# Half a tile of tokens moved from matmuls over all experts to dots over fetched rows

## The chip, the cores and the metric

The kernel runs on one core of one Trainium2 chip. The metric is the device time of one execution, in microseconds. An execution computes one transformer layer over 512 tokens.

## The reference

The layer mixes 512 tokens of 1024 features with four kinds of attention, normalises, and then runs an expert layer (PEER) with 16384 experts, each one row of `u` and one row of `v`. Each token picks 16 experts in each of 8 heads, 128 in all, through two lists of 128 subkeys:

```python
s_top, i_top = lax.top_k(sub, PEER_TOPK)                 # 16 of 128, in both halves of a head
cand = s_top[:, :, 0, :, None] + s_top[:, :, 1, None, :]
sc, ci = lax.top_k(cand.reshape(t_len, PEER_HEADS, 256), PEER_TOPK)
eid = (i1 * N_KEYS + i2).reshape(t_len, 128)
gate = jax.nn.softmax(sc, axis=-1).reshape(t_len, 128)
...
h = jax.nn.gelu(jnp.einsum('cd,ced->ce', xc, u[ec]), approximate=False)
return jnp.einsum('ce,ced->cd', gc * h, v[ec])
```

The result is normalised once more. The change concerns the expert layer alone.

## The kernel before

**Data.** Tokens lie in four tiles of 128. Weights come in units of 128 x 1024 numbers (0.524 MB). SP loads each unit into one of four slots of `raw` (`load_unit`); ScalarE rounds it to `w_hi` (`split_hi`, L539); GpSimd or DVE takes the remainder `w_lo` (L486, L1055). TensorE makes three matmuls of each product, high by high, high by low and low by high.

**The expert layer in two halves.** For tiles 1 to 3 (384 tokens) the kernel computes all 16384 experts. First half: 128 units of `u`, each eight chunks by three matmuls with 384 token columns (`project`, L1285 to L1287) into PSUM bank 0 or 1 in turn. ScalarE applies gelu from there (`gelu_of`) and stores the result to the DRAM scratch `gelu_d`. Second half: 128 units of `v` (`value_unit`, `add_tile`, L1511 to L1514), for each tile six matmuls with 512 columns. Their stationary operand is gate times gelu, which DVE multiplies (`times_gelu`) from `gate_in` and `gelu_in` as they come back from DRAM, and which is split again (`gh_high` on ScalarE, `gh_low` on DVE).

For tile 0 only the chosen experts are computed. GpSimd fetches rows of `u` by index (`get_u`, 128 rows of 4 KB a fetch, 0.524 MB), DVE multiplies each by the token's x, which stands in PSUM banks 6 and 7, and sums (`dot`, L1061): 128 dots in the first half. In the second half rows of `v` are fetched (`get_v`) and added with their weights (`fma`, L1073).

**The gates.** DVE picks the experts of a tile (`route`: runs of MAX8, FIND_INDEX8, MATCH_REPLACE8, then a selection in PSUM banks 2 to 5). TensorE turns the picks (`turn_picks`), DVE copies them (`spread_picks`, L1169). Then the tile goes four tokens (a quad) at a time: DVE builds two indicator matrices `left` and `match` of 128 x 512 (`mark`, L1179 and L1180), DVE or, for three quads of four, ScalarE makes `right` from `match` and the gates, TensorE multiplies them per token (`gates_of`, L1609), ScalarE copies the 128 x 128 gates of four tokens to `stage` (`take_gates`, L731), and after eight quads stores 2 MB of them to `gate_d` (`store_gates`, L738).

**Order.** Every engine's order is written out by hand, along the 128 units of the first half: 16 units alone, then three times (tiles 1, 2, 3) 14 units during which the tile is routed and 16 units in which two quads follow each unit, then 22 units of tail. `dots_by` says how many dots are done by which unit: 3, 6, 6 in the routing stretches, 30 in each marking stretch, 23 in the tail. DVE does the marks of a unit, then the dots due by it, in one order; GpSimd does a unit's split, then the fetches due (up to five dots ahead, one buffer each). A fetch waits until the dot that used its buffer is done. In the tail SP starts to reload the gates at unit 120 (`load_gates`), after the last store has landed.

## Time and profile before

| | |
|---|---|
| median of 3 runs | 1729.89 us (1728.78 to 1734.46) |
| the profiled execution | 1732.18 us |
| its span, first to last instruction | 1730.4 us |
| TensorE busy | 1689.1 us (98%) |
| VectorE (DVE) busy | 1255.8 us (73%) |
| ScalarE (ACT) busy | 768.7 us (44%) |
| GpSimd (POOL) busy | 820.7 us (47%) |
| moved by DMA | 417.65 MB, mean 241 GB/s |
| first half of the expert layer | about 580 to 1197 us |
| second half | 1197 to 1718 us |

Busy time is an average over stages with different limits, so the stages are read one by one. Matmul durations in the profile are modelled and overlap; the pace is read from one start to the next. Idle time of an engine that isn't the bound costs nothing; what it waited for tells what would be late next. The granted TensorE clock is 1.00 (2.4 GHz) in all stretches of the expert layer.

### The profile page before, as it was taken

Reading aid. Unit: us, or ns where it says so; the run is one execution under the profiler, and the core shown is the slowest. Engines: PE = TensorE matmul, PEld = TensorE weight load, DVE = VectorE, ACT = ScalarE, POOL = GpSimd, SP = SyncE. Lnnn points to the kernel's source line nnn. Section 1 sums busy time; section 2 is a strip of 40 time slices with the busy share of each in tenths; the row PEclk is TensorE's granted clock in tenths of the full one; section 3 lists DMA queues with packets and bytes.
Section 4 is the critical chain, followed back from the end, with each engine's and each line's share of the span. In section 5 each row is a group of like instructions: output and inputs, shape, how many; then the busy total and the mean of one; then the engine's idle time right before and its main releaser. Section 6 shows DMA issues by size and latency. Waiting matters only on the chain.

```text
span 1730.4 us, 24570 instructions
## 1 busy us (share of the span) xinstructions
PE 1689.1 (98%) x9061; PEld 1486.3 (86%) x9061; DVE 1255.8 (73%) x2490; ACT 768.7 (44%) x1301; POOL 820.7 (47%) x496
## 2 busy tenths in 40 slices
PE   7999999999999999999999999999999999999997
PEld 6667767778878999999999999999888888888886
DVE  2487896562353778789888987534888888888886
ACT  4444444522232443775577367534333333333332
POOL 5222222344446466766777677776433232332312
PEclk9999999999999999999999999999999999999998
DMA  5111111224233365899799789997999999999952
GB/s 200 61 62 50 59 60 54 77 94 146 84 112 110 113 197 186 306 372 345 253 333 384 249 286 386 383 364 296 405 390 354 384 376 351 383 372 354 389 190 85
DMA packets 126360, 417.65 MB, mean 241 GB/s; under 512 B 12961, under 2 KB 32417, under 8 KB 124705
## 3 DMA queue, kind: packets, MB, share of 16 engines
q1 hardware_dynamic: 70176, 232.81, 38.2%
...
## 4 chain that ended last, share of the span: by engine, by line
PE 88%; DVE 8%; ACT 2%; issue 1%; DMA 1%; POOL 0%; SPq 0%; another core or an unknown queue 0%; ACTq 0%; DVEq 0%; POOLq 0%
PE ps L1285 16%; PE ps L1287 16%; PE ps L1286 16%; PE ps L1514 11%; PE ps L1511 11%; PE ps L1512 11%; PE ps L1609 5%; PE ps L1370 1%; DVE dist_a L842 1%; DVE row L895 1%; DVE row L866 1%; DVE small L841 1%; PE ps L1395 1%; DVE small L892 1%; DMA raw<-w_units 0%
## 5 line engine op out<-in xcount | busy, mean ns | idle before, releaser
L1285 PE MATMUL ps<-tok_hi,w_hi 128*128 128x384 f32 (+2 forms) x1544 | 548.8, 355 | 8.4 <-issue 3.6
L1287 PE MATMUL ps<-tok_hi,w_lo 128*128 128x384 f32 (+2 forms) x1544 | 539.3, 349 | 0.0
L1286 PE MATMUL ps<-tok_lo,w_hi 128*128 128x384 f32 (+2 forms) x1544 | 539.3, 349 | 0.0
L539 ACT ACTIVATE w_hi<-raw 128x1024 fp32r<-128x1024 f32 x334 | 353.3, 1058 | 414.0 <-PE ps L1514 301.4
L486 POOL TENSOR_TENSOR w_lo<-raw,w_hi 128x1024 fp32r<-128x1024 f32 x128 | 318.2, 2489 | 165.8 <-ACT w_hi L539 165.2
L439 POOL TENSOR_TENSOR w_lo<-raw,w_hi 128x1024 fp32r<-128x1024 f32 x80 | 195.0, 2442 | 327.0 <-ACT w_hi L539 326.8
L1285 PEld LDWEIGHTS ps<-tok_hi,w_hi 128*128 128x128 f32 x1544 | 291.1, 189 | 35.7 <-issue 10.2
L1287 PEld LDWEIGHTS ps<-tok_hi,w_lo 128*128 128x128 f32 x1544 | 290.8, 188 | 18.6
L1286 PEld LDWEIGHTS ps<-tok_lo,w_hi 128*128 128x128 f32 x1544 | 291.3, 189 | 16.8
L1511 PE MATMUL ps<-w_hi,gh_hi 128*128 128x512 f32 x768 | 298.8, 389 | 0.0
L1512 PE MATMUL ps<-w_lo,gh_hi 128*128 128x512 f32 x768 | 298.8, 389 | 0.0
L503 POOL DMA_INDIRECT v_got<-v_rows,eid x128 | 150.4, 1175 | 303.6 <-DVE own L1073 286.7
L1514 PE MATMUL ps<-w_hi,gh_lo 128*128 128x512 f32 x768 | 236.5, 389 | 0.0
L1061 DVE CUSTOM_DVE_ANT_0 u_got<-u_got,ps 128x1024 f32<-128x1024 f32 x128 | 153.3, 1217 | 90.5 <-DMA u_got<-u_rows,eid 88.0
L1055 DVE TENSOR_TENSOR w_lo<-raw,w_hi 128x1024 fp32r<-128x1024 f32 x126 | 156.3, 1241 | 74.0 <-ACT w_hi L539 73.4
L1514 PEld LDWEIGHTS ps<-w_hi,gh_lo 128*128 128x128 f32 x768 | 144.2, 188 | 29.9
L1512 PEld LDWEIGHTS ps<-w_lo,gh_hi 128*128 128x128 f32 x768 | 144.2, 188 | 29.9
L1511 PEld LDWEIGHTS ps<-w_hi,gh_hi 128*128 128x128 f32 x768 | 144.2, 188 | 29.8
L1073 DVE SCALAR_TENSOR_TENSOR own<-v_got,w_own,own 128x1024 f32<-128x1024 f32 x126 | 159.8, 1278 | 0.0
L495 POOL DMA_INDIRECT u_got<-u_rows,eid x128 | 123.1, 961 | 27.7 <-issue 20.4
L706 ACT ACTIVATE gelu_t<-ps 128x384 f32<-128x384 f32 x120 | 58.7, 489 | 173.3 <-PE ps L1287 151.5
L1609 PE MATMUL ps<-right,left 128*128 128x128 f32 x768 | 93.5, 275 | 0.5 <-ACT right L722 0.5
...
## 6 DMA issues: line engine op xcount, KB each, us to landing
raw<-u_units SPq DMA_DIRECT2D x128, 512.0 KB
raw<-v_rows SPq DMA_DIRECT2D x128, 512.0 KB
...
gelu_d<-gelu_t ACTq DMA_DIRECT2D x120, 192.0 KB
...
```

Of the source, the lines that this page charges most:

```text
L439: pool.tensor_tensor(w_lo[:, n % RAW, :], raw[:, n % RAW, :], w_hi[:, n % RAW, :].bitcast(F32), ALU.subtract).then_inc(lo_done, 1)
L486: pool.tensor_tensor(w_lo[:, n % RAW, :], raw[:, n % RAW, :], w_hi[:, n % RAW, :].bitcast(F32), ALU.subtract).then_inc(lo_pool, 1)
L539: act.activation(w_hi[:, n % RAW, :], raw[:, n % RAW, :], ACT.Copy).then_inc(hi_done, 1)
L1055: dve.tensor_tensor(w_lo[:, n % RAW, :], raw[:, n % RAW, :], w_hi[:, n % RAW, :].bitcast(F32), ALU.subtract).then_inc(lo_dve, 1)
L1073: dve.scalar_tensor_tensor(own[e % 2][:], v_got[e % V_SLOTS][:], w_own[:, e:e + 1], own[e % 2][:], ALU.mult, ALU.add).then_inc(fma_done, 1)
L1285: pe.matmul(out_, l_hi, r_hi, start=start, stop=False)
L1286: pe.matmul(out_, l_hi, r_lo, start=False, stop=False)
L1287: return pe.matmul(out_, l_lo, r_hi, start=False, stop=stop)
L1511: pe.matmul(o, l_hi[:, tile_], wh, start=start, stop=False)
L1512: pe.matmul(o, l_hi[:, tile_], wl, start=False, stop=False)
L1514: last = pe.matmul(o, l_lo[:, tile_], wh, start=False, stop=stop)
L1609: last = pe.matmul(ps[:, 2 + q % 3, t * P:(t + 1) * P], left[:, s, t, :], right[:, s, t, :], start=True, stop=True)
```

## The change

The first 64 tokens of tile 1 (`NEAR`) leave the first half's matmuls, which now have 320 columns (`UT`). Their h is computed by dots instead. Two groups of 64 experts lie on the two halves of the partitions, so 64 more dots cover 64 tokens times 128 experts; 192 dots in all (`DOTS`). Their indices, x rows and results are spread and brought back by six small DMAs on ScalarE's queue (`spread_near_eid`, `spread_near_x`, `finish_near`). The x in PSUM is exchanged before dot 42 and again before dot 106 (`take_x`). The gates of these tokens are multiplied by their gelu (`weigh_near`) and marked last, after tile 3, for which their picks are kept and turned a fourth time; the second half then multiplies them by ones (`gelu_in[:, :, 0:NEAR]`), since it still covers all three tiles.

The order is new. 14 units alone, then three times 18 units of routing, and 9, 17 and 25 units of marking with 16, 32 and 48 quads; a tail of 9 units. Dots: 8, 10, 10 in routing, 22, 44, 68 in marking, 6 in the tail, 24 in the first 16 units of the second half (`late_dots_by`). Fetches may use three buffers before the ninth dot, then five, and six in the middle (`slots_at`, `dot_slots`). Two quads are marked in one instruction with 1024 elements. In the second half, one unit of four is split by GpSimd instead of DVE (`by_pool`), the fmas start at unit 18 instead of 2 and end at 118 instead of 116, and tile 3 is summed in banks 0 and 1, as banks 6 and 7 hold x. The first reload of gates stands behind the last `u` unit, its second part behind the second `v` unit.

```diff
-FIRST_UNITS, ROUTE_UNITS, MARK_UNITS = 16, 14, 16
-TAIL = FIRST_UNITS + 3 * (ROUTE_UNITS + MARK_UNITS)
-ROUTE_DOTS, MARK_DOTS = (3, 6, 6), 30
-U_SLOTS, V_SLOTS = 5, 6
-FMA_START, FMA_END = 2, P - 12
+NEAR = 2 * TOK
+UT = DT - NEAR
+NEAR_GROUPS = P // NEAR
+DOTS = P + NEAR
+FIRST_UNITS, ROUTE_UNITS, MARK_UNITS = 14, 18, (9, 17, 25)
+TAIL = FIRST_UNITS + 3 * ROUTE_UNITS + sum(MARK_UNITS)
+ROUTE_DOTS, MARK_DOTS, TAIL_DOTS, LATE_DOTS = (8, 10, 10), (22, 44, 68), 6, 24
+NEAR_FROM, NEAR_END = 42, 42 + NEAR
+assert sum(ROUTE_DOTS) + sum(MARK_DOTS) + TAIL_DOTS + LATE_DOTS == DOTS
+U_SLOTS, V_SLOTS = 6, 6
+FMA_START, FMA_END = LATE_DOTS * 2 // 3 + 2, P - 10
...
+def routed_at(b):
+
+    return FIRST_UNITS + (b - 1) * ROUTE_UNITS + sum(MARK_UNITS[:b - 1])
+
+
+def first_quad(b):
+
+    return max(0, 32 * (b - 1) - NEAR // 4) if b < NT else N_QUAD
+
+
+def tile_quad(q):
+
+    r = q + NEAR // 4
+    return r // 32 + 1, r % 32
+
+
+def quads_of(b, k):
+
+    first, count = first_quad(b), first_quad(b + 1) - first_quad(b)
+    return range(first + count * k // MARK_UNITS[b - 1], first + count * (k + 1) // MARK_UNITS[b - 1])
+
+
+def pairs_of(b, k):
+
+    return [q for q in quads_of(b, k) if q % 2 == 0]
...
+def stretch_dots():
+
+    by = [0] * FIRST_UNITS
+    for b in range(1, NT):
+        for units, dots in ((ROUTE_UNITS, ROUTE_DOTS[b - 1]), (MARK_UNITS[b - 1], MARK_DOTS[b - 1])):
+            by += [by[-1] + dots * (k + 1) // units for k in range(units)]
+    units = P - TAIL
+    return by + [by[-1] + TAIL_DOTS * (k + 1) // units for k in range(units)]
...
+DOTS_BY = stretch_dots()
+NEAR_UNIT = next(k for k in range(P) if DOTS_BY[k] >= NEAR_END) + 3
+
+
+def dot_row(d):
+
+    if NEAR_FROM <= d < NEAR_END:
+        return True, d - NEAR_FROM
+    return False, d if d < NEAR_FROM else d - NEAR
...
+def slots_at(d):
+
+    return 3 if d < ROUTE_DOTS[0] else U_SLOTS if SIX_FROM <= d < SIX_END else U_SLOTS - 1
...
+def fmas_by(j):
+
+    return max(0, min(P, P * (j - FMA_START + 1) // (FMA_END - FMA_START)))
+
+
+def late_dots_by(j):
+
+    return min(DOTS, DOTS - LATE_DOTS + 3 * (j + 1) // 2)
+
+
+DOT_SLOTS = dot_slots()
+
+
+def by_pool(j):
+
+    return j + LO_AHEAD < P and j % 4 == 1
...
+                j = n - first - P
+                if by_pool(j):
+                    engine.wait_ge(lo_pool, P + sum(by_pool(i) for i in range(j + 1)))
+                else:
+                    engine.wait_ge(lo_dve, sum(not by_pool(i) for i in range(j + 1)))
+
+    def ffn_bank(t):
+
+        return {1: 2, 2: 4, 3: 0}[t]
...
             for j in range(P):
                 load_unit(U_EXP + j, u_units[j])
-                if j == P - 8:
-                    sp.wait_ge(gate_read, N_QUAD)
-                    for s in range(2):
-                        sp.wait_ge(stage_out[s], 16 * (NB // 2))
-                    load_gates(0, 0)
-                if j == P - 4:
-                    load_gates(0, 1)
+            sp.wait_ge(gate_read, N_QUAD)
+            for s in range(2):
+                sp.wait_ge(stage_out[s], 16 * (NB // 2))
+            load_gates(0, 0)
             for j in range(P):
                 load_unit(U_VAL + j, v_rows[:, (j - KEPT) % P, :])
+                if j == 1:
+                    load_gates(0, 1)
...
+                if k == P - 8:
+                    pool.wait_ge(pick_set, NT)
+                    pool.wait_ge(dot_done, SIX_END)
+                    for i in range(2):
+                        pool.memset(gelu_in[i][:, :, 0:NEAR], 1.0).then_inc(ones_set, 1)
+                if k < FIRST_UNITS + ROUTE_UNITS:
+                    rows_to(min(DOTS_BY[k - 1] + 3, ROUTE_DOTS[0]))
+                else:
+                    done = DOTS_BY[k - 1]
+                    rows_to(done + slots_at(done))
             for s in range(2):
...
-            for e in range(P):
-                get_v(e)
+            sent = 0
+            for j in range(P):
+                if by_pool(j):
+                    expert_lo(P + j)
+                rows_to(late_dots_by(j) + U_SLOTS - 1)
+                while sent < min(P, fmas_by(j - 1) + V_SLOTS):
+                    get_v(sent)
+                    sent += 1
             pool.wait_ge(ln2_in, 32)
...
+            def spread_near_eid():
+
+                act.wait_ge(near_set, 1)
+                for g in range(NEAR_GROUPS):
+                    part = slice(NEAR * g, NEAR * g + NEAR)
+                    act.dma_start(near_eid[part, :], near_all[0:NEAR, part]).then_inc(near_eid_in, 16)
+
+            def spread_near_x():
+
+                act.wait_ge(pick_set, 3)
+                for g in range(NEAR_GROUPS):
+                    act.dma_start(near_x[NEAR * g:NEAR * g + NEAR, :], x_tok[0:NEAR, 1, :]).then_inc(near_x_in, 16)
+
+            def finish_near():
+
+                act.wait_ge(dot_done, NEAR_END)
+                act.activation(near_dot[:], near_dot[:], ACT.Gelu).then_inc(near_gelu, 1)
+                act.wait_ge(near_gelu, 1)
+                for g in range(NEAR_GROUPS):
+                    part = slice(NEAR * g, NEAR * g + NEAR)
+                    act.dma_start(near_h[0:NEAR, part], near_dot[part, :]).then_inc(near_h_in, 16)
 
             for k in range(FIRST_UNITS):
                 expert_unit(k)
@@ -750,17 +884,25 @@
...
+            def take_x(rows, n):
+
+                dve.wait_ge(dot_done, n)
+                dve.tensor_copy(ps[:, 6:8, :].rearrange("p a n -> p (a n)"), rows).then_inc(own_x, 1)
+                dve.wait_ge(own_x, 2 if n == NEAR_FROM else 3)
...
+            def keep_near():
+
+                dve.wait_ge(pick_set, 2)
+                dve.scalar_tensor_tensor(near_all[:], pick[:, 0, :], float(NK), pick[:, 1, :], ALU.mult, ALU.add)\
+                    .then_inc(near_set, 1)
+                dve.tensor_copy(near_keys[:], pick[:, 0:2, :])
+                settled(dve.tensor_copy(near_gate[:], pick[:, 2, :]))
+
+            def weigh_near():
+
+                dve.wait_ge(near_h_in, 16 * NEAR_GROUPS)
+                dve.tensor_tensor(near_gate[0:NEAR, :], near_gate[0:NEAR, :], near_h[0:NEAR, :], ALU.mult)\
+                    .then_inc(near_pick, 1)
+
...
             def mark(q):
 
-                s, quad = q % 4, q % 32
+                b, quad = tile_quad(q)
                 if q >= 4:
-                    dve.wait_ge(gate_full, q - 3)
-                first, second, gate = (ps[:, 5, a * P + 4 * quad:a * P + 4 * quad + 4].unsqueeze(2).to_broadcast([P, 4, P])
-                                       for a in range(3))
-                numbers = iota[:].unsqueeze(1).to_broadcast([P, 4, P])
-                dve.tensor_tensor(left[:, s, :, :], numbers, first, ALU.is_equal)
-                dve.tensor_tensor(match[:, s, :, :], numbers, second, ALU.is_equal).then_inc(match_set, 1)
-                if right_by(q)[0] == "dve":
-                    dve.wait_ge(match_set, q + 1)
-                    dve.tensor_tensor(right[:, s, :, :], match[:, s, :, :], gate, ALU.mult).then_inc(right_dve, 1)
+                    dve.wait_ge(gate_full, q - 2)
+                first, second = (ps[:, 5, a * P + 4 * quad:a * P + 4 * quad + 8].unsqueeze(2).to_broadcast([P, 8, P])
+                                 for a in range(2))
+                numbers = iota[:].unsqueeze(1).to_broadcast([P, 8, P])
+                two = slice(q % 4, q % 4 + 2)
+                dve.tensor_tensor(left[:, two, :, :].rearrange("p s t k -> p (s t) k"), numbers, first, ALU.is_equal)
+                dve.tensor_tensor(match[:, two, :, :].rearrange("p s t k -> p (s t) k"), numbers, second, ALU.is_equal)\
+                    .then_inc(match_set, 1)
+                if right_by(q + 1)[0] == "dve":
+                    gate = ps[:, 5, 2 * P + 4 * quad + 4:2 * P + 4 * quad + 8].unsqueeze(2).to_broadcast([P, 4, P])
+                    dve.wait_ge(match_set, q // 2 + 1)
+                    dve.tensor_tensor(right[:, 3, :, :], match[:, 3, :, :], gate, ALU.mult).then_inc(right_dve, 1)
 
             def times_gelu(j):
 
@@ -1189,6 +1366,8 @@
...
+                for k in range(MARK_UNITS[b - 1]):
                     expert_unit(routed_at(b) + ROUTE_UNITS + k)
-                    for quad in (2 * k, 2 * k + 1):
-                        gates_of(32 * (b - 1) + quad)
+                    for quad in quads_of(b, k):
+                        if b == NT - 1 and tile_quad(quad) == (NT, 0):
+                            turn_picks(NT)
...
-                tokens = slice(P, S) if n >= U_EXP else slice(0, S)
-                to = ps[:, bank, 0:DT] if n >= U_EXP else ps[:, bank, :]
+                tokens = slice(P + NEAR, S) if n >= U_EXP else slice(0, S)
+                to = ps[:, bank, 0:UT] if n >= U_EXP else ps[:, bank, :]
...
+                if b == NT:
+                    pe.wait_ge(near_pick, 1)
+                    pe.wait_ge(match_set, (N_QUAD - NEAR // 4) // 2)
+                    pe.wait_ge(right_dve, (N_QUAD - NEAR // 4) // 4)
+                    pe.wait_ge(gate_full, N_QUAD - NEAR // 4)
+                else:
```

## Rows read from the trace of the kernel before

**Rows 1.** The page's chain that ended last, shares by engine and by line

```profile
PE 88%; DVE 8%; ACT 2%; issue 1%; DMA 1%; POOL 0%; SPq 0%; another core or an unknown queue 0%; ACTq 0%; DVEq 0%; POOLq 0%
PE ps L1285 16%; PE ps L1287 16%; PE ps L1286 16%; PE ps L1514 11%; PE ps L1511 11%; PE ps L1512 11%; PE ps L1609 5%; PE ps L1370 1%; DVE dist_a L842 1%; DVE row L895 1%; DVE row L866 1%; DVE small L841 1%; PE ps L1395 1%; DVE small L892 1%; DMA raw<-w_units 0%
```

**Rows 2.** Groups of instructions by shape (count, busy us, mean ns), TensorE

```profile
L1285 PE MATMUL ps<-tok_hi,w_hi 128*128 128x384 f32 x1024 | 346.5, 338 | 0.0
```

**Rows 3.** Timeline (start us, us), TensorE: 256-column matmuls, then the first of 384

```profile
532.09 0.28 PE L1287 MATMUL ps<-tok_hi,w_lo 128*128 128x256 f32 x1
...
540.01 0.28 PE L1287 MATMUL ps<-tok_hi,w_lo 128*128 128x256 f32 x1
...
580.49 0.34 PE L1285 MATMUL ps<-tok_hi,w_hi 128*128 128x384 f32 x1
```

**Rows 4.** The chain in order of time (start us, us): marking, first value matmul

```profile
724.43 1.78 PE ps L1609 x16
...
795.79 1.78 PE ps L1609 x16
...
1196.88 0.23 PE ps L1511
```

**Rows 5.** Windows: PE, PEld, DVE, ACT, POOL busy, granted clock, DMA share, GB/s

```profile
712.00:800.00 88.00, 87.75 (x591) 87.75 (x592) 77.44 (x156) 62.88 (x143) 65.20 (x45) 1.00 0.98 376
...
1020.00:1108.00 88.00, 88.00 (x595) 88.00 (x594) 72.44 (x122) 62.81 (x142) 63.45 (x44) 1.00 0.96 361
...
1400.00:1600.00 200.00, 200.00 (x884) 165.64 (x883) 171.22 (x203) 72.24 (x98) 61.76 (x55) 1.00 0.99 369
```

**Rows 6.** The same view in windows of 20 us

```profile
1020.00:1040.00 20.00, 20.00 (x141) 20.00 (x140) 19.38 (x34) 15.16 (x35) 14.09 (x11) 1.00 0.87 290
1040.00:1060.00 20.00, 20.00 (x134) 20.00 (x134) 14.22 (x25) 14.15 (x32) 13.82 (x11) 1.00 1.00 389
1060.00:1080.00 20.00, 20.00 (x137) 20.00 (x136) 17.41 (x31) 14.91 (x36) 14.53 (x10) 1.00 1.00 393
...
1140.00:1160.00 20.00, 20.00 (x117) 20.00 (x116) 6.21 (x12) 5.53 (x8) 16.10 (x11) 1.00 1.00 371
...
1240.00:1260.00 20.00, 20.00 (x89) 16.54 (x89) 17.85 (x23) 8.71 (x12) 10.48 (x7) 1.00 1.02 405
```

**Rows 7.** Groups of instructions, DVE, 1020 to 1108 us, with idle before

```profile
L1061 DVE CUSTOM_DVE_ANT_0 u_got<-u_got,ps 128x1024 f32<-128x1024 f32 x30 | 35.8, 1215 | 15.3 <-DMA u_got<-u_rows,eid 15.2
```

**Rows 8.** Timeline of DVE: two mark steps, a dot, routing of tile 2

```profile
789.20 0.68 DVE L1179 TENSOR_TENSOR left<-iota,ps 128x512 f32<-128x512 f32 x1
789.80 0.68 DVE L1180 TENSOR_TENSOR match<-iota,ps 128x512 f32<-128x512 f32 x1
...
793.45 1.22 DVE L1061 CUSTOM_DVE_ANT_0 u_got<-u_got,ps 128x1024 f32<-128x1024 f32 x1
...
794.60 3.19 DVE L1083 MAX8 s_top<-sub 128x8 f32<-128x128 f32 x16
...
850.62 0.29 DVE L1160 TENSOR_TENSOR pick<-pick,g_sum 128x128 f32<-128x128 f32 x1
856.19 0.29 DVE L1169 COPY g_T<-ps 128x128 f32<-128x128 f32 x1 [5.28 <-PE ps L1598]
```

**Rows 9.** Groups of instructions, GpSimd, 1020 to 1108 us

```profile
L486 POOL TENSOR_TENSOR w_lo<-raw,w_hi 128x1024 fp32r<-128x1024 f32 x15 | 36.1, 2404 | 18.2 <-ACT w_hi L539 18.1
L495 POOL DMA_INDIRECT u_got<-u_rows,eid x29 | 27.4, 944 | 6.4 <-issue 4.6
```

**Rows 10.** Timeline of ScalarE around the last store of gates

```profile
1111.26 0.33 ACTq L738 DMA_DIRECT2D gate_d<-stage  x1
...
1113.93 0.33 ACTq L708 DMA_DIRECT2D gelu_d<-gelu_t  x1
...
1124.42 0.49 ACT L706 ACTIVATE gelu_t<-ps 128x384 f32<-128x384 f32 x1 [4.85 <-DMA gelu_d<-gelu_t]
```

**Rows 11.** Groups of instructions, DVE, 1200 to 1400 us

```profile
L1055 DVE TENSOR_TENSOR w_lo<-raw,w_hi 128x1024 fp32r<-128x1024 f32 x50 | 61.1, 1223 | 28.2 <-ACT w_hi L539 27.6 <-issue 0.6
```

199 lines of the change are left out of this document (122 added, 77 removed).

## The prediction

> **What bounds the kernel now.** I read the chain of work that ended last first [rows 1]: 88% of the span is TensorE, and the lines of the two expert halves (L1285 to L1287, L1511 to L1514, L1609) carry nearly all of it. So a shorter TensorE stream is worth its whole length, until another engine is late. Then the rates of the matmuls. Their durations in the groups of instructions [rows 2] are modelled and overlap, so I take start to start: 0.120 us at 256 columns in the same line of code [rows 3] (66 matmuls from 532.09 to 540.01), and 200/884 = 0.226 at 512 columns [rows 5]. For 384 columns the chain gives 5.947 us for a unit with eight gate matmuls (12 periods from 724.43 to 795.79) [rows 4]; less 1.78 for the gates that is 4.165, or 0.1735 us for each of 24. The three lie on one line, 0.42 ns a column. Last, who is close behind. In the stretches in which gates are marked, DVE is busy 77.4 of 88 us, and the DMA engines 0.96 to 0.98 of the time at 361 to 376 GB/s [rows 5]; already there dots wait 15.3 us for fetched rows in 88 us [rows 7]. The kernel is bound by TensorE, with DMA at its heels in just the stretches to which the change adds transfers.
>
> **What the change takes off TensorE.** 3 x 1024 matmuls [rows 2] go from 384 to 320 columns: 0.1735 - 64 x 0.00042 = 0.147 us, 3.52 us a unit for 4.165. 128 units x 0.64 = 82 us. The 96 quads of gate matmuls stay (0.89 each, 85 us); three transposes more are 0.5 us. Before, the last first-half unit ends at 1196.88 [rows 4]; TensorE alone would bring that to 1115. The second half (18 matmuls of 512 columns, 4.07 us a unit) keeps its length.
>
> **DVE.** Dots cost 1.14 us from their start to that of the next instruction (793.45 to 794.60, read of the sum and all) [rows 8]. 64 are added and 24 of the 192 lie in the second half, so 168 instead of 128 in the first: +46 us. A mark step is 0.60 us for 512 elements, start to start (789.20 to 789.80) [rows 8]; at 1.04 ns an element (0.53) a step of 1024 costs 1.13, so the joined steps save 0.07 x 96 = 6 us. Route: from the first MAX8 at 794.60 to the last of pick at 850.9 is 56.3, of which 6 dots are 6.9 [rows 8]; 49.4 without. With 8, 10, 10 dots: 59, 61, 61 us; 18 units of TensorE are 63.4, so routing stays just hidden. The three mark stretches have 16, 32, 48 quads, 22, 44, 68 dots, and 9, 17, 25 units. A pair of quads is 2.27, right for every second pair 0.7 more: DVE needs 46, 92 and 141 us, plus some 2.5 us each in the last two for copying the new x rows (1.2 each) and the picks of the late tokens. TensorE needs 9 x 3.52 + 16 x 0.89 = 46, 88 and 131. So DVE becomes some 16 us longer than TensorE over these. Adding up from 580.49 (first 384-column unit after unit 0) [rows 3], less 0.6: unit 31 ends at 689; marks to 736; route to 799; marks to 895; route to 959; marks to 1103; nine units of tail 32: 1135 by DVE. To that comes one hand-over that the trace of before has only at the start of a mark stretch: at the 33rd quad of the third stretch DVE waits in spread_picks until TensorE has finished the 17 units and 32 quads before and one unit more and turned the picks of the late tokens (all marks and dots behind it wait too), then TensorE waits for the first new right. Before, DVE stood 5.3 us at the like place [rows 8], where it had run ahead; I take 4, bounds 0 and 7: 1139.
>
> **The other new waits and small DMAs.** near_eid, near_x and near_h are two small transfers each on ScalarE's queue, 0.33 us an issue [rows 10], 2 us over 450. finish_near holds ScalarE (behind it: the next split and gelu, and so TensorE's banks) until 106 dots are done, but it stands three units, 16 us, after they are planned, and near_h has nine units to arrive before weigh_near. Nothing, as long as dots are less than 16 us late. The first copy of near_x waits for all dots before it, which is DVE's own order. SP's gate reload moves from unit 120 to behind the last u unit; by the tail's account below it couldn't run earlier.
>
> **GpSimd.** A split is 2.40, a gather's issue 0.94 and some 0.2 of idle between issues [rows 9]. A mark unit with 2.7 dots: 2.40 + 2.7 x 1.15 = 5.5 us, where TensorE has 5.24 and DVE 5.6. It is a third resource at the same length, on no path by itself. Its in-order waits for dot_done hold the next split, but a split is two units ahead, 10 us.
>
> **DMA.** From 689, when rows after the eighth can be fetched, to the end of the first half, must move: 93 units of u and 4 of v (50.9 MB, 0.524 each), 160 gathers (83.9), gelus of 88 units at 0.164 (14.4), the gates out (25.2) and the first of them in (3.1), x rows 0.5: 178 MB. What does DMA carry? Fully busy 20 us windows moved 389 and 393 GB/s in marking, 371 in the tail, 405 in the second half [rows 6]; whole stretches 361 to 376 [rows 5]. I take 390, that of the same mixture, since in the long stretches part of the time was ramp (290 GB/s at 1020 to 1040 [rows 6]). 178/0.390 = 456 us, which ends at 1145. Two route stretches can't fill it: each has some 22.4 MB for 62 us, 57 at 390, so 9 us more. Row waits that DVE can't hide now that it has no slack: 8 us, an estimate of half of one stretch's 15.3 [rows 7], and 2 for the hand-over, where transfers run on; bounds 0 and 1/6 of the mark time (48). End of the first half: 1164. So DMA, not TensorE, is late: a mark unit has 2.56 MB, 6.6 us at 390 against 5.24.
>
> The tail shrinks from 22 units (92 us) to nine (32 us), with the last gate store and the gates' reload in it. A gelu store queued behind the gate store of 1111.26 frees its buffer at 1124.4, so a store takes ScalarE's queue some 12 us [rows 10]. After it the reload (3.1 MB, 8 us at full rate, 16 at half), then gh, its high and low parts (2 us): 22 to 30 us after ACT's last take, which lies 28 us before the end. It is inside the 178 MB; beyond it I take 1 us, bounds 0 and 12. The same store holds gelu buffers when units are 3.5 us long: two banks cover 10.6 us of those 12.
>
> **Second half.** By bytes, the first 16 units have 0.524 + 1.5 x 0.524 + 0.164 + 0.197 = 1.67 MB in 4.07 us, 410 GB/s, later ones 382 (before: 370). At 400, 1.6 us late; at the 369 of today's second half [rows 5], which is its demand and perhaps not its limit, 7 us. DVE there: per unit 1.5 dots (1.7), 0.75 of a split (1.22 [rows 11], 0.9), two half-microsecond steps: 3.6 of 4.07. The splits on GpSimd are needed two units later, 8 us, so nothing. The gate tile waits for banks 0 and 1 once, under 1 us. Together I take +3 us, bounds 0 and 17.
>
> **Sum** against the profiled execution, 1732.2 us (span 1730.4; the median of the runs is 2.3 lower): 1165 for 1197 is -32, second half +3: 1703. I keep that number; the 2.3 is below what I can resolve.
>
> The DMA rate is the doubtful term, and a rule speaks against mine. Fully busy windows here moved 371 to 405 GB/s on one core [rows 6]. The Trainium skill (HBM Reference, Specifications (TRN2)) has some 358 GB/s as a core's effective share of memory bandwidth, and more for a core alone. By 358 the first half would end at 689 + 497 + 10 = 1196, no gain at all; by its single-core figure of about 425 (same section), 689 + 419 + 19 = 1127, under DVE's 1139. The windows are all above the share.
>
> **Rivals.** (a) DMA keeps up and DVE or TensorE sets the pace. For it: windows of 393 to 405 [rows 6]. Against: dots wait today with fewer rows [rows 7]. End at 1139 to 1145: 1677 to 1683. Chance 0.2. (b) Each row wait of today comes on top of DVE's work instead of vanishing in its slack, since gate stores take the queues in bursts: 15.3/88 of 284 us is 49; 1139 + 49 - 6 (waits that fall where TensorE is late anyway) is 1182, total 1720. Chance 0.2. (c) The slower side: three queues at once push the rate to that of the whole stretch at 361 GB/s, or lower [rows 5]. 178/0.361 = 493, so 1182 + 10 of coupling + 5 at the turn = 1197, and the second half, which needs 382, gets the 369 of today and loses 17 us over 480: 1749. It decides below 370 GB/s. Against: fully busy windows of the first half moved 371 at the least [rows 6]. The per-core share of 358 would land here too, by rule. Chance 0.08. (d) The shorter matmul doesn't shorten the period, because weight loads set it: then the end stays at 1197 and all is 1731. Against: 256 columns ran at 0.120 with the same loads [rows 3]. Chance 0.03. Forecast: 0.49, own range 1689 to 1713.
>
> **Numbers.** 1703 us. The range leaves out (c), (d) and the edges: 1672 to 1725. Faster by over 0.3% (some 5 us, about what a measurement of this kernel can tell): 0.49 + 0.2 + 0.18 = 0.87; the same 0.06; slower 0.07.
>
> **What would show it.** Right: 24 matmuls in 3.52 us in the tail; a mark unit of 6 to 6.6 us instead of 5.24; DMA share 0.98 or more through the three mark stretches; gate matmuls that wait for right, and DVE that waits for u_got over 20 us in the last stretch; last first-half unit at about 1165. Wrong: mark units of 5.3 to 5.7 with short row waits (then (a)), an end near 1182 with DMA share under 0.95 (then (b)), or TensorE waiting inside the second half for gh_lo (my 3 us).

## The result, and the profile after

The changed kernel takes 1781.55 us (median of 4 runs, 1778.72 to 1786.21). The kernel before, on the same chip, takes 1731.26. The ratio is 1.0297 (95% interval 1.0273 to 1.0321): 50 us slower, where 28 us faster was forecast.

I cut each profiled execution at the first weight load for a value matmul, since the two halves are limited by different things. "Start" below is that moment, and "second half" is the rest of the span. Both come from one execution of each kernel; the time in us given with a ratio is the median of several.

| | span | start | second half |
|---|---|---|---|
| before | 1730.4 | 1196.5 | 533.9 |
| forecast | 1701 | 1165 | 537 |
| after | 1780.7 | 1230.1 | 550.6 |

The first half got 34 us longer instead of 32 shorter, and the second 17 longer instead of 3. The page of after answers [rows 1] with this (the span, busy time of each engine, then the chain that ended last by engine):

```profile
span 1780.7 us, 24705 instructions
PE 1647.1 (92%) x9064; PEld 1434.0 (81%) x9064; DVE 1363.2 (77%) x2497; ACT 766.1 (43%) x1302; POOL 1011.8 (57%) x594
PE 58%; DVE 18%; DMA 9%; POOL 6%; issue 5%; ACT 2%; ACTq 0%; SPq 0%; DVEq 0%; POOLq 0%
```

TensorE had 88% of the chain and has 58%: it no longer sets the time alone. What it waits for in the first half stands in the groups of instructions of TensorE from 689 to 1225 us (count, busy us, mean ns, then idle before and its releaser):

```profile
L1470 PE MATMUL ps<-tok_hi,w_hi 128*128 128x320 f32 x765 | 248.7, 325 | 26.0 <-POOL w_lo L573 25.7 <-ACT gelu_in L812 0.2
L1801 PE MATMUL ps<-right,left 128*128 128x128 f32 x768 | 110.8, 299 | 46.3 <-ACT right L833 46.0
L1790 PE MATMUL ps<-ident,pick 128*128 128x128 f32 x6 | 1.4, 354 | 5.4 <-DVE pick L1320 5.4
```

That is 77.7 us of waits in a stretch where TensorE had practically none before. With 5.1 us at the turn to the second half it is 83. The start lies 115 us behind what the shorter matmuls alone would give (1230 against 1115), so 32 us are left that are no waits. The trace puts nearly all of them down to the clock. From 689 us to the start the granted clock is 0.92 in the mean, and since it has two levels (1.2 and 2.4 GHz), that is 86 of 541 us at the lower one. TensorE worked in 56 of these 86, so it lost 28 us by them; the other 30 fell into waits. In the timeline of TensorE (start, duration, and in brackets the idle time before it) the matmuls after a wait run at half rate:

```profile
739.75 3.79 PE L1801 MATMUL ps<-right,left 128*128 128x128 f32 x16 [8.00 <-ACT right L833]
...
743.60 0.47 PE L1471 MATMUL ps<-tok_lo,w_hi 128*128 128x320 f32 x1
743.87 0.47 PE L1472 MATMUL ps<-tok_hi,w_lo 128*128 128x320 f32 x1
...
744.62 0.31 PE L1472 MATMUL ps<-tok_hi,w_lo 128*128 128x320 f32 x1
744.77 0.31 PE L1470 MATMUL ps<-tok_hi,w_hi 128*128 128x320 f32 x1
744.91 0.31 PE L1471 MATMUL ps<-tok_lo,w_hi 128*128 128x320 f32 x1
```

After 8.00 us of idle the 16 gate matmuls take 3.79 us instead of 1.78 [rows 4]. Matmuls of 320 columns then start every 0.27 us, and from 744.6 every 0.147. The granted clock is 0.50 from 735 to 740, 0.55 from 740 to 745 and 1.00 from there. So TensorE worked some 5 us at 1.2 GHz after the wait before 2.4 GHz came back. The windows over the four parts of the first half (PE, PEld, DVE, ACT, POOL busy, granted clock, DMA share, GB/s) show it in the mean:

```profile
700.00:820.00 120.00, 93.07 (x632) 91.83 (x631) 104.80 (x289) 54.39 (x101) 74.83 (x48) 0.88 0.76 276
820.00:940.00 120.00, 108.27 (x737) 106.59 (x736) 89.62 (x123) 72.43 (x162) 93.77 (x68) 0.93 0.98 366
940.00:1060.00 120.00, 105.53 (x710) 104.18 (x709) 118.04 (x292) 58.72 (x106) 87.81 (x53) 0.96 0.82 294
1060.00:1180.00 120.00, 100.82 (x678) 97.76 (x676) 95.12 (x134) 70.93 (x164) 83.54 (x64) 0.91 0.98 377
```

Before, the clock column was 1.00 in each of these windows and PE busy 119.5 to 120.0. The DMA columns matter too: 366 and 377 GB/s at a share of 0.98 in the two parts that mark, but 276 and 294 in the two in which most of a routing stage lies. At a share of 0.98 the marking parts have little room to make up for it.

### The profile page after: what moved, and what is told of

Read it like the earlier page. It is cut to its first block, busy times and chain, and to the rows that moved or that the text cites. A ratio compares the mean times of both kernels' runs of the same rounds, so it can differ in the third digit from the quotient of the medians.

```text
span 1780.7 us, 24705 instructions
## 1 busy us (share of the span) xinstructions
PE 1647.1 (92%) x9064; PEld 1434.0 (81%) x9064; DVE 1363.2 (77%) x2497; ACT 766.1 (43%) x1302; POOL 1011.8 (57%) x594
## 4 chain that ended last, share of the span: by engine, by line
PE 58%; DVE 18%; DMA 9%; POOL 6%; issue 5%; ACT 2%; ACTq 0%; SPq 0%; DVEq 0%; POOLq 0%
PE ps L1696 10%; PE ps L1699 10%; PE ps L1697 10%; PE ps L1470 9%; PE ps L1472 8%; PE ps L1471 8%; DMA u_got<-u_rows,eid 4%; DVE u_got L1217 4%; POOL w_lo L573 3%; POOL u_got L589 2%; DMA u_got<-u_rows,near_eid 2%; DMA gelu_in<-gelu_d 2%; PE ps L1801 1%; PE ps L1555 1%; DVE match L1355 1%
## 5 line engine op out<-in xcount | busy, mean ns | idle before, releaser
L1470 PE MATMUL ps<-tok_hi,w_hi 128*128 128x320 f32 (+2 forms) x1544 | 530.5, 344 | 34.7 <-POOL w_lo L573 25.7
L1471 PE MATMUL ps<-tok_lo,w_hi 128*128 128x320 f32 (+2 forms) x1544 | 519.6, 337 | 0.0
L1472 PE MATMUL ps<-tok_hi,w_lo 128*128 128x320 f32 (+2 forms) x1544 | 518.3, 336 | 0.0
L573 POOL TENSOR_TENSOR w_lo<-raw,w_hi 128x1024 fp32r<-128x1024 f32 x160 | 393.6, 2467 | 145.6 <-ACT w_hi L647 144.0
L526 POOL TENSOR_TENSOR w_lo<-raw,w_hi 128x1024 fp32r<-128x1024 f32 x80 | 194.9, 2440 | 325.5 <-ACT w_hi L647 325.3
L597 POOL DMA_INDIRECT v_got<-v_rows,eid x128 | 202.7, 1584 | 119.9 <-DVE own L1230 94.0
L1217 DVE CUSTOM_DVE_ANT_0 u_got<-u_got,ps 128x1024 f32<-128x1024 f32 x192 | 227.7, 1217 | 56.2 <-DMA u_got<-u_rows,eid 43.5
L1230 DVE SCALAR_TENSOR_TENSOR own<-v_got,w_own,own 128x1024 f32<-128x1024 f32 x126 | 187.2, 1504 | 0.0
L1801 PE MATMUL ps<-right,left 128*128 128x128 f32 x768 | 110.8, 299 | 46.3 <-ACT right L833 46.0
L1801 PEld LDWEIGHTS ps<-right,left 128*128 128x128 f32 x768 | 102.3, 209 | 52.7 <-ACT right L833 52.2
L1375 DVE TENSOR_TENSOR gh<-gate_in,gelu_in 128x384 f32<-128x384 f32 x128 | 91.4, 715 | 66.9 <-DMA gelu_in<-gelu_d 38.9
```

The lines of the kernel that those rows point to most:

```text
L526: pool.tensor_tensor(w_lo[:, n % RAW, :], raw[:, n % RAW, :], w_hi[:, n % RAW, :].bitcast(F32), ALU.subtract).then_inc(lo_done, 1)
L573: pool.tensor_tensor(w_lo[:, n % RAW, :], raw[:, n % RAW, :], w_hi[:, n % RAW, :].bitcast(F32), ALU.subtract).then_inc(lo_pool, 1)
L597: pool.indirect_dma_start(out=v_got[e % V_SLOTS][:], out_offset=None, in_=v_rows.rearrange("p a d -> (p a) d"), in_offset=bass.IndirectOff ...
L1217: dve.tensor_tensor_reduce(out=u_got[slot][:], in0=u_got[slot][:], in1=ps[:, 6:8, :].rearrange("p a n -> p (a n)"), scale=1.0, scalar=0.0, ...
L1470: pe.matmul(out_, l_hi, r_hi, start=start, stop=False)
L1471: pe.matmul(out_, l_hi, r_lo, start=False, stop=False)
```

## The experiments

Three things were suspected in the first half: a wait on GpSimd, rows that land late, and a routing stage that is longer than its instructions. Each was taken away alone and then together.

**1. GpSimd's wait for the picks (e1_six).** GpSimd gets the sixth row buffer at dot SIX_FROM, and asks first whether the picks of tile 2 are done, because the buffer lies where routing works. In its queue that wait stands ahead of the low parts of the next weights. The timeline of GpSimd in after:

```profile
785.76 4.78 POOL L573 TENSOR_TENSOR w_lo<-raw,w_hi 128x1024 fp32r<-128x1024 f32 x2
813.89 0.95 POOL L589 DMA_INDIRECT u_got<-u_rows,eid  x1 [23.36 <-DVE pick L1320]
814.87 2.35 POOL L573 TENSOR_TENSOR w_lo<-raw,w_hi 128x1024 fp32r<-128x1024 f32 x1
```

TensorE, two units behind, runs dry: it is busy for 2.64 us in the window from 800 to 820. The edit lets the wait come after the five rows that do not need the buffer.

```diff
-SIX_FROM = DOTS_BY[routed_at(2) + ROUTE_UNITS - 1]
+SIX_FROM = DOTS_BY[routed_at(2) + ROUTE_UNITS - 1] + U_SLOTS - 1
```

> The changed kernel with one number altered: the sixth fetch buffer comes into use five dots later, so that GpSimd's wait for the picks of tile 2 is reached only in the second marking stretch. In the trace of the changed kernel GpSimd stands 23 us in that wait at 790 to 814 us with the next weight split queued behind it, and TensorE 19 us. Theory A (the in-order wait on GpSimd is a cause by itself): TensorE's gap of 19 us goes, the first half ends 20 to 28 us earlier, the total is about 1757. Rival B (the DMA engines or DVE set the pace over the whole first half, so the gap is filled by what is late anyway): the later stretches take back most of it, under 8 us gained, total about 1775.

Measured: 1767.28 us (ratio 1.0214, 1.0197 to 1.0231), start 1213.2. The wait for w_lo falls from 25.7 us to 8.5. So this one line of order costs 14 us of time and 17 of the first half: less than the 20 to 28 of theory A, more than the 8 of rival B. One reason shows in the timeline of DVE. Routing of tile 2 took 66.6 us in after and takes 76.8 in e1_six, since GpSimd now works beside all of it (part 5 has what that does). The runs below that name e1_six are built on it.

**2. The columns alone (e2_cols).** The kernel before with 320 columns and nothing else; the 64 tokens' h is left out.

```diff
-                tokens = slice(P, S) if n >= U_EXP else slice(0, S)
-                to = ps[:, bank, 0:DT] if n >= U_EXP else ps[:, bank, :]
+                tokens = slice(P + 64, S) if n >= U_EXP else slice(0, S)
+                to = ps[:, bank, 64:DT] if n >= U_EXP else ps[:, bank, :]
```

> The kernel before with 320 instead of 384 columns in the first expert matmuls and nothing else; the h of 64 tokens is left out (stale values take its place), so no dots, fetches or exchanges are added, and the old schedule stays. It measures the term of the sum that the prediction took as 82 us. If TensorE is all that binds, 1731 - 82 = 1650. If the old number of dots (DVE 0.88 busy in marking, DMA 0.98) already stands behind it, the marking stretches shrink by less: DMA needs 2.2 MB a unit, 5.6 us at 390 GB/s where TensorE would need 5.3, so some 10 to 20 us less gain, about 1665.

Measured: 1708.53 us (0.9872, 0.9855 to 0.9888), start 1171.4. Of the 82 us that TensorE saves, 25 reach the start of the second half even with no dot added; both expected times, 1650 and 1665, were far too low. TensorE waits 46 us, 31.7 of them for the picks at the end of two routing stages: 14 units of 3.52 us are 49, and routing takes 64.4 and 64.5 here, against 56.3 and 56.6 before, with the two-input instructions of part 5 held beside GpSimd's splits. The rows are not what got worse: dots wait 82.7 us for them, 88.0 before. So under the old order most of the saving was not on offer, whatever the dots cost. The changed kernel has 18 units to a routing stage and not 14, so this run does not bound what it could gain.

**3. The rows of the near tokens (e3_nofetch, e7_six_nofetch).** The 64 added fetches are left out, and the dots work on stale rows. e3 is built on the changed kernel, e7 on e1_six.

```diff
+                if near:
+                    return
...
-                dve.wait_ge(u_in[slot], 16 * use)
+                if not near:
+                    dve.wait_ge(u_in[slot], 16 * use)
```

> The changed kernel with the 64 fetches for the new dots left out (the dots run on what stands in the buffer, so the h of these tokens is not computed); DVE does all its dots, GpSimd issues 64 fetches less, DMA moves 33.5 MB less. Theory A (row fetches through busy DMA engines hold DVE, and by that TensorE): the second and third marking stretch run near DVE's own 5.6 us a unit, and the total falls by 35 to 60 us, to 1720 to 1745. Rival B (DVE's work and the in-order waits are the cause, not the transfers): within 10 us of the changed kernel, about 1775.

> Both edits together: the sixth buffer's wait moved into the second marking stretch, and the 64 fetches for the new dots left out (their h is not computed). Each alone took 14 and 31 us off the total. If the wait on GpSimd and the transfers are causes side by side, together 45 us: total about 1737, first half ending at 1181 instead of 1230. If both stand for the same lost time (GpSimd's queue late in the second marking stretch), together under 38: above 1743. DVE's own sum of the prediction would end the first half at 1139; what is left above it is neither of the two.

Measured: 1750.72 (1.0116, 1.01 to 1.0133), start 1197.8; and 1745.8 (1.0093, 1.0076 to 1.011), start 1193.4. The 33.5 MB of rows cost 32 us of the first half with the GpSimd wait in place and 20 without it. The two causes overlap, as the second case of e7's expectation has it (above 1743); e3 gained 31 us where at least 35 was expected.

**4. All the bytes of rows (e8_quarter).** e1_six with a quarter of each u row fetched and used four times, so the chosen experts' h are other numbers. The number of requests, dots and waits is the same.

```diff
-                    out=u_got[slot][:], out_offset=None, in_=u_rows,
+                    out=u_got[slot][:, 3 * DM // 4:], out_offset=None,
+                    in_=u_rows.rearrange("e (q d) -> (e q) d", q=4),
```

> The changed kernel with the sixth buffer's wait moved, and each fetch of u rows (all 192) cut to a quarter of a row, which the dot reads four times over (so h is not what the reference has); every instruction and wait stays, DMA moves 75 MB less. If transfers hold DVE, the row waits (43 us) go almost entirely and the first half ends 50 to 70 us earlier than the 1213 of the kernel with the moved wait alone, near DVE's own 1139 plus hand-overs, about 1150. If the dots wait mostly for GpSimd, which issues the fetches between its splits, the waits stay above 20 us and the first half ends above 1175.

Measured: 1721.77 (0.9954, 0.9941 to 0.9967), start 1176.3, 37 us earlier than e1_six. Waits of dots for rows between 689 and the start of the second half fall to 12 us; after had 48 there, e1_six 42. So these waits come from the bytes of the rows and not from the number of requests. But the start came down to 1176 and not to the 1150 expected, so something else holds DVE. The edit takes three quarters of all 192 rows away, also of the 128 that the kernel before fetches, so 37 us is not the price of the added ones.

**5. What holds the routing stage (e9_smallsplit).** Routing with 10 dots was forecast at 61 us. From the first MAX8 to the end of the last write of pick it takes 66.6 and 77.1 in after. In the timeline of DVE, while tile 3 is routed in after, two small instructions stand out:

```profile
967.48 5.08 DVE L1260 TENSOR_TENSOR cand<-s_top 128x128 f32<-128x128 f32 x1
972.49 0.61 DVE L1262 TENSOR_TENSOR cand<-s_top 128x448 f32<-128x448 f32 x1
...
982.90 5.47 DVE L1282 TENSOR_TENSOR pick<-c_top 128x128 f32<-128x128 f32 x1
```

and in GpSimd's of the same time:

```profile
967.66 4.75 POOL L573 TENSOR_TENSOR w_lo<-raw,w_hi 128x1024 fp32r<-128x1024 f32 x2
...
979.88 2.42 POOL L573 TENSOR_TENSOR w_lo<-raw,w_hi 128x1024 fp32r<-128x1024 f32 x1
...
983.43 4.78 POOL L573 TENSOR_TENSOR w_lo<-raw,w_hi 128x1024 fp32r<-128x1024 f32 x2
```

The two DVE instructions of 128 elements take 0.29 us when undisturbed. Here each ends within 0.2 us of the end of a pair of GpSimd splits, though its record begins 0.2 to 0.5 us before the pair does, while GpSimd issues a row request (966.69 to 967.64 and 982.45 to 983.40). The trace of after has three more instructions held in this way, one of them the c_col instruction of tile 3: 7.01 us, where 2.29 is undisturbed. The edit makes the splits short (8 of 1,024 columns) in the routing units of tiles 2 and 3; the low parts of those weights are stale.

```diff
+                cols = slice(0, 8 if any(routed_at(b) <= k < routed_at(b) + ROUTE_UNITS for b in (2, 3)) else DM)
-                pool.tensor_tensor(w_lo[:, n % RAW, :], raw[:, n % RAW, :], w_hi[:, n % RAW, :].bitcast(F32),
+                pool.tensor_tensor(w_lo[:, n % RAW, cols], raw[:, n % RAW, cols], w_hi[:, n % RAW, cols].bitcast(F32),
```

> Left out: GpSimd's low-part splits of the routes for tiles 2 and 3 work on 8 of 1,024 columns, so the low parts of those weights are stale; everything else is as in e1_six. Theory of the lock (VectorE instructions that start beside a GpSimd split stand until it ends): the two route stages of tiles 2 and 3 take about 61 us instead of 75, and the time falls by 15 to 28 us from e1_six, to 1740 to 1752. Rival, that the stages are held by rows that the transfers bring late: less than 5 us, 1762 to 1768.

Measured: 1741.69 (1.0071, 1.0048 to 1.0093), start 1186.9, 26 us earlier than e1_six. Both routing stages take 56.7 us, measured as above, where e1_six has 76.8 and 77.1. The short splits also relieve GpSimd: TensorE's waits for w_lo in the first half, 8.5 us in e1_six, are gone. Those waits fall into routing stages too, and no run parts the held DVE instructions from GpSimd's own shorter queue. The rival, late rows, is not what changed: dots wait 46 us for rows here and 42 in e1_six. The groups of instructions of DVE from 689 us to the start of the second half, first of after, then of e9_smallsplit:

```profile
L1282 DVE TENSOR_TENSOR pick<-c_top 128x128 f32<-128x128 f32 x2 | 10.9, 5454 | 0.1
L1260 DVE TENSOR_TENSOR cand<-s_top 128x128 f32<-128x128 f32 x2 | 10.2, 5100 | 0.0
L1303 DVE TENSOR_TENSOR ps<-c_col,iota 128x2048 f32<-128x2048 f32 x2 | 9.3, 4652 | 0.0
```

```profile
L1304 DVE TENSOR_TENSOR ps<-c_col,iota 128x2048 f32<-128x2048 f32 x2 | 4.6, 2294 | 0.0
L1283 DVE TENSOR_TENSOR pick<-c_top 128x128 f32<-128x128 f32 x2 | 0.6, 292 | 0.1
L1261 DVE TENSOR_TENSOR cand<-s_top 128x128 f32<-128x128 f32 x2 | 0.6, 286 | 0.0
```

Three lines give back 24.6 us over two stages. The dots do not change (1.22 us beside a split or not): one of their two inputs lies in PSUM. The Trainium skill (SBUF — State Buffer, Who interferes with whom) says that a VectorE instruction with two SBUF inputs contends with a GpSimd instruction that reads SBUF. The Trainium skill (the same page, Summary: rules for kernel authors) adds that the second one to issue blocks fully until the first has finished. The trace agrees in which DVE instructions are held and which are not. It does not show that order or that length: DVE's records begin before those of the splits, and the wait covered two splits in a row (5.08 and 5.47 us beside pairs of 4.75 and 4.78).

**6. Both together (e18_both).** The edits of parts 4 and 5 on e1_six.

> e8_quarter and e9_smallsplit in one: quarter rows fetched (a dot takes one quarter four times, so the experts' results are other ones) and 8-column splits on GpSimd in the routes of tiles 2 and 3. If waits for rows and held route instructions are two causes that add, the first half ends 20 to 28 us before e8_quarter's 1176, at 1148 to 1156 (by the prediction's sum for VectorE 1139), and the time is 1692 to 1702. If they are one cause counted twice, it stays within 8 us of e8_quarter: 1714 to 1724.

Measured: 1695.67 (0.9812, 0.9796 to 0.9829), start 1148.9, 27 us before e8_quarter. The two causes add, as the first case expected. The steps of the first half are then: 1230.1 in after, 1213.2 without GpSimd's wait for the picks, 1176.3 without three quarters of the rows' bytes, 1148.9 with short splits in routing. The last step contains both the freed route instructions and TensorE's waits for w_lo, 11.7 us of the first half in e8_quarter and none in e18_both. The forecast's sum for DVE was 1139. In e18_both TensorE's waits in the first half are down to 20 us, nearly all for right:

```profile
L1805 PE MATMUL ps<-right,left 128*128 128x128 f32 x768 | 104.1, 285 | 20.0 <-ACT right L835 19.3
```

**7. The 2 MB stores (e4_paced).** The changed kernel with each gate store, but the last, in four parts over three units.

```diff
+                    store_part(body, 0)
+                    late_stores.append([(body, 1)])
+                    late_stores.append([(body, 2), (body, 3)])
```

> The changed kernel with each 2 MB store of gates cut into four of 0.5 MB, issued over three units; the same bytes. Theory A1 (bursts: while 2 MB stand in ScalarE's queue the fetches get a share too small, five buffers run empty and DVE waits up to 8 us): the row waits shrink to under half of their 43 us, total 15 to 30 us less, 1750 to 1765. Rival A2 (the mean rate is what is short): no change within 5 us.

Measured: 1774.2 (1.0247, 1.023 to 1.0264), 7 us less than after. That fits rows that stand behind a large store: dots wait 40 us for rows where after has 48. It is less than the 15 to 30 us that theory A1 had, and just over the 5 us of its rival.

**8. The second half (e5_dvesplit, e6_nolate).** e5 gives GpSimd's splits of the second half back to DVE (`by_pool` always false). e6 leaves out the 24 late fetches, and their dots work on stale rows.

```diff
-    return j + LO_AHEAD < P and j % 4 == 1
+    return False
```

```diff
+                if d >= DOTS - LATE_DOTS:
+                    return
```

> The changed kernel with all weight splits of the second half on DVE again instead of one in four on GpSimd. In the changed kernel the fmas of the second half take 1504 ns on average, before 1278, and gh products 715, before 550. Theory S1 (DVE instructions that begin while GpSimd is in a split stand until it ends): with no splits on GpSimd the fmas fall back below 1300 ns and the second half, 550.6 us long there and 533.7 before, loses 5 to 15 us, although DVE has 39 us of splits more. Rival S2 (DVE has no room for them): the second half becomes longer by 10 us or more. Theory S3 (it is the transfers): fmas shorter, the total unchanged within 4 us.

> The changed kernel with the fetches of the 24 late dots left out (those dots run on what stands in the buffer, so their h is not computed); 12.6 MB less at the start of the second half, the same work on DVE. Theory S3 (the transfers of the first 16 units are what delays the gelu blocks and v units there): the second half goes from 550.6 to about 540 us, total 10 us less, about 1771. Rival S1 or S2 (locks and DVE's load): under 3 us less.

Measured: e5 1777.73 (1.0274, 1.0257 to 1.0291), second half 551.4; e6 1764.83 (1.0208, 1.0191 to 1.0225), second half 537.3. Here are the groups of DVE in the second half, of after and then of e5_dvesplit (each time the scaled rows of v, then gh):

```profile
L1230 DVE SCALAR_TENSOR_TENSOR own<-v_got,w_own,own 128x1024 f32<-128x1024 f32 x126 | 187.2, 1504 | 0.0
...
L1375 DVE TENSOR_TENSOR gh<-gate_in,gelu_in 128x384 f32<-128x384 f32 x126 | 90.4, 717 | 39.6 <-DMA gelu_in<-gelu_d 38.9
```

```profile
L1230 DVE SCALAR_TENSOR_TENSOR own<-v_got,w_own,own 128x1024 f32<-128x1024 f32 x126 | 158.7, 1278 | 0.0
...
L1375 DVE TENSOR_TENSOR gh<-gate_in,gelu_in 128x384 f32<-128x384 f32 x126 | 71.6, 568 | 22.3 <-DMA gelu_in<-gelu_d 22.3
```

GpSimd's splits hold DVE here too (1504 ns against 1278), yet without them the half is as long: it was not on the path, as theory S3 has it. What is on the path are the transfers. In after the chain from 1250.5 runs through two loads of gelu_in that take 14.85 and 15.88 us to land, at 367 GB/s with a DMA share of 0.98 from 1250 to 1420; TensorE is busy 164.63 of those 170 us. In e6 the share is 0.89 and TensorE busy 169.28. The 12.6 MB of late rows cost 13 of the 17 us by which the second half grew.

**9. The order of marks and dots (e10_ahead), of requests (e12_lag, e14_lead).** All on e1_six. e12 (first diff) asks for a row two units later in GpSimd's order, e14 (second) one unit earlier, and e10 (third) puts marks one unit ahead of dots.

```diff
-                    done = DOTS_BY[k - 1]
+                    done = DOTS_BY[k - 3]
```

```diff
-                    done = DOTS_BY[k - 1]
+                    done = DOTS_BY[min(k, P - 1)]
```

```diff
+                marks = [(k, quad) for k in range(MARK_UNITS[b - 1]) for quad in pairs_of(b, k)]
...
-                    for quad in pairs_of(b, k):
+                    while marks and marks[0][0] <= k + 1:
```

> e1_six with VectorE's marks (the matches that TensorE needs) put one unit ahead of the dots. Theory that the order on VectorE carries a late row on to TensorE: TensorE's waits for right, 37.6 us in e1_six, fall by half and the time by 10 to 25 us, to 1743 to 1757. Rival, that the sum of transfers sets the pace of the first half: less than 5 us, 1762 to 1768.

> e1_six with one change of order on GpSimd: the row of a dot is asked for two units later, so that GpSimd stands less before a dot that VectorE has not reached (10.15 us at 981.73 in e1_six) and its splits no longer run in pairs of 4.8 us. Theory that the in-order waits for dots bunch the splits, and the bunched splits hold VectorE: the route stages of tiles 2 and 3 shorten from 75 to 62 to 68 us and the time falls by 8 to 20 us, to 1747 to 1759. Rival, that the splits hold VectorE whatever their order: within 5 us of e1_six (1762 to 1772), or slower, up to 1785, because each row comes two units later.

> e1_six with each dot's row asked for one unit earlier in GpSimd's order (e12_lag, two units later, took 215 us more). Theory of the ring (request, landing, dot, mark, scaled match, gate matmul, high part, low part, request: a step of it that comes later comes back to itself): one unit earlier shortens the waits for rows, and the time falls by 5 to 25 us, to 1742 to 1762. Rival: in e1_six the ring is already free, GpSimd only stands longer before dots that VectorE has not done, with its splits behind it: 1767 to 1785.

Measured: e10 1765.61 (1.0198, 1.0181 to 1.0215) and e14 1765.17 (1.0202, 1.0185 to 1.0219): no difference from e1_six. e12 1981.77 (1.1457, 1.1405 to 1.1509): 215 us more. e12 was expected between 1747 and 1785. Its routing stages did shorten, to 69.5 and 61.9 us from 76.8 and 77.1, but dots now wait 285 us for rows in the first half, and why the splits bunch in e1_six is left open. What e12 shows is a ring. The chain of e12_lag in order of time (start, us):

```profile
1118.31 2.41 POOL w_lo L573
1120.72 0.14 issue
1120.86 0.95 POOL u_got L589
1121.81 0.30 issue
1122.11 12.28 DMA u_got<-u_rows,eid
...
1134.53 1.22 DVE u_got L1217
1135.76 1.13 DVE left L1354
1136.89 1.14 DVE match L1355
...
1138.36 0.98 ACT right L833 x3
...
1139.39 2.09 PE ps L1801 x8
...
1142.00 1.06 ACT w_hi L647
1143.06 0.07 issue
1143.13 2.41 POOL w_lo L573
1145.54 0.15 issue
1145.70 0.95 POOL u_got L589
```

A low part, a request, the landing, a dot, the marks behind it, the scaling, the gate matmuls, the next high part, the next low part, the next request: 24.8 us a turn. The request stands behind the low part only by GpSimd's order. In e1_six, as in after, it goes out two units earlier, and one unit earlier still (e14) gains nothing, so there the ring does not set the pace.

**10. Half as many tokens (e11_32, e13_combo, e15_32_nolate, e16_paced32, e17_32_paced).** e11 is e1_six with 32 tokens taken out (352 columns) and 12 late dots. e15 puts those 12 into the first half and leaves GpSimd no splits in the second; e16 is e15 with the paced stores; e17 is e11 with them. e13 is e15 with the requests of e12.

```diff
-NEAR = 2 * TOK
+NEAR = TOK
...
+FIRST_UNITS, ROUTE_UNITS, MARK_UNITS = 14, 18, (13, 17, 21)
...
+ROUTE_DOTS, MARK_DOTS, TAIL_DOTS, LATE_DOTS = (6, 8, 8), (26, 40, 54), 6, 12
```

> e1_six with 32 tokens taken out of the matmuls instead of 64 (352 columns), their dots spread the same way. If the fetched rows' transfers cost more than the columns save, the time moves toward the kernel before in proportion: between 1740 and 1755, half-way from e1_six (1767) to before (1730), with a few us less for the shorter routes. If it is a threshold (DMA saturates only with the full 64), about 1715 to 1730, at or below the kernel before.

> e11_32 with no dots and no GpSimd splits in the second half, the same later requests as in e12_lag, and the 12 late dots done in the first half. If the late rows are what the second half pays, its length goes from 545 back to 534 to 537; the first half takes the 12 dots (14 us of VectorE, 6.3 MB of transfers = 16 us at 390 GB/s) and loses between 2 and 12 us. Sum: 1733 to 1744, and at or below 1731 only if the later requests give back over 5 us.

> e11_32 without dots and without GpSimd splits in the second half, the 12 dots done in the first half, and the requests in their first order (so e13_combo without its later requests). Second half 534 to 537 us instead of 545; the first half takes the 12 dots and their 6.3 MB, 2 to 12 us. Sum 1733 to 1744. A time below 1731 would say that the first half had room for them.

> e15_32_nolate with the gate store in four parts over three units, as in e4_paced, where it gave 7 us. If rows wait behind the 2 MB store, 3 to 8 us below e15_32_nolate; if with half the rows the store does not matter, within 2 us of it.

> e11_32 with its gate store in four parts over three units. If the pacing adds as in e16_paced32 (16 us below e15_32_nolate), 1727 to 1735, level with the kernel before (1730); if it adds as in e4_paced (7 us), 1735 to 1739; if e11_32, with 12 dots fewer in the first half, has no rows late behind a store, 1741 to 1745.

| | us | ratio | start | second half |
|---|---|---|---|---|
| e11_32 | 1743.40 | 1.0082 (1.0054 to 1.0111) | 1190.7 | 544.8 |
| e13_combo | 1978.48 | 1.1426 (1.1386 to 1.1466) | 1438.7 | 540.3 |
| e15_32_nolate | 1757.62 | 1.0144 (1.0123 to 1.0164) | 1220.6 | 539.2 |
| e16_paced32 | 1741.60 | 1.0061 (1.0042 to 1.008) | 1196.7 | 539.6 |
| e17_32_paced | 1735.27 | 1.0029 (1.0013 to 1.0045) | 1186.0 | 544.6 |

e13 is the ring again. e11 lies half-way from e1_six to the kernel before, as expected of a cost in proportion. The runs of e11 spread from 1737 to 1753 us, and its profiled one is 6 us under the median while that of e15 is 4 over, so the medians tell more here than the starts. By them twelve dots moved from the second half to the first cost 14 us net (e15 against e11), though the second half gives 6 back; e15 was expected at 1733 to 1744. Pacing the stores is worth 16 us in e16 (3 to 8 were expected), 8 in e17 and 7 in e4, with 160, 148 and 168 dots in the first half: no order by how full that half is. The best version, e17, is 10 us faster in the first half than before and 11 slower in the second. None of these five beats the kernel before.

## Why the prediction was wrong, point by point

**TensorE's saving: right.** 320-column matmuls start every 0.147 us, as worked out. What the saving was worth was another matter: e2_cols shows 25 of the 82 us even without added dots.

**"In-order waits for dot_done hold the next split, but a split is two units ahead": the step that failed first.** The paragraph on GpSimd priced its issues and its waits for dots, and never the new wait for the picks of tile 2 that the diff adds to the same function. It stands at the end of a routing stage, 23.4 us, where the prediction's lead was 10 us and two units of 3.52 us are 7. That cost 17 us of the first half (e1_six).

**DVE's sum of 1139: 10 us short, plus 27 that it had no term for.** e18_both starts the second half at 1148.9, with 12 us of waits for rows left in it; its routing stages take 56.8 and 56.7 where 61 was summed, so the shortfall lies in the marking and the hand-over. (The "some 16 us" by which DVE was to outlast TensorE in marking are 19 by the terms given; the 1139 has them in full.) The routing stages were costed from one stage before [rows 8], in which some 3 us collided; with 10 dots beside GpSimd's splits they became 77 us, and short splits give 27 us of the first half back (e18_both against e8_quarter), part of it perhaps by way of GpSimd's shorter queue. The trace of before hinted at it: the route instruction on c_col (L1143) averages 3.0 us there over the last two stages, where 2.3 is undisturbed.

**DMA: late rows hold DVE, as forecast, but the size was not right.** I took 390 GB/s, 9 us for routes that can't fill it and 8 us of row waits. Rival (b) charged 49 us for the last. Three quarters of the rows' bytes cost 37 us on top of e1_six (e8_quarter). Here is after by its own stages (tile 2 routed and marked, tile 3 routed and marked), then two short windows of the last:

```profile
746.00:814.00 68.00, 52.63 (x363) 52.37 (x361) 66.87 (x235) 26.38 (x36) 36.10 (x21) 0.92 0.63 224
814.00:944.00 130.00, 113.43 (x764) 111.52 (x765) 93.59 (x129) 75.08 (x168) 102.49 (x73) 0.91 0.96 359
944.00:1022.00 78.00, 65.60 (x434) 64.70 (x433) 76.98 (x235) 30.70 (x41) 55.89 (x30) 0.97 0.77 270
1022.00:1200.00 178.00, 155.22 (x1041) 151.97 (x1041) 148.54 (x208) 106.57 (x246) 126.58 (x97) 0.91 0.96 365
...
1060.00:1080.00 20.00, 16.58 (x121) 15.94 (x120) 17.50 (x24) 13.41 (x33) 16.28 (x14) 1.00 1.04 404
1080.00:1100.00 20.00, 15.29 (x104) 14.68 (x103) 15.27 (x24) 11.46 (x29) 12.30 (x9) 0.90 1.01 408
```

Short windows reach 404 and 408 GB/s, but 390 was too high for whole marking stages, which moved 359 and 365 at a share of 0.96. The two routing stages moved 36 MB in 146 us, where I had 45 MB in 124. With five or six row buffers, a row is fetched only as a dot finishes, and DVE was held there; this link is read off the order and not tested by itself. So the mistake was to take the best windows for the rate of a stage, and to count routing as nearly full. The mean of the half, 331 GB/s, is no more than the same bytes over the longer time and explains nothing by itself. The Trainium skill (HBM Reference, Specifications (TRN2)) has the share of 358 GB/s a core that was weighed against the forecast, and as an estimate by it the half would have ended at 1196. That is nearer than my 1165, but the windows of 404 and 408 lie above the share, and the routing stages far below it.

**Clock: no term.** I counted a wait as its own length. With the clock at half rate for some microseconds after many of them, 83 us of waits cost 115: 28 of the 32 us between are TensorE's work at 1.2 GHz, by the granted clock in the trace. No run changed the clock alone.

**The turn: inside its bounds.** TensorE waits 5.1 us for gh_lo; 1 was taken, bounds 0 and 12.

**The second half: 17 us at the upper bound, for 3.** The bytes of the late rows account for 13 of them (e6_nolate), and after moves 367 GB/s from 1250 to 1420, close to the 369 of rival (c); the splits on GpSimd do cost DVE time, off the path (e5_dvesplit).

**The chances.** Rival (c) is the nearest in time, and its rates did come: 361 GB/s forecast for the first half, 359 and 365 measured in marking, and 367 in the second. But it ends at 1749 and not at 1781, since the emptier routing stages, the in-order wait, the held instructions and the fallen clock were missing from it as from every case. That several terms err the same way was given almost no chance (slower: 0.07).
